# A decoder layer on one core: the next pair's tokens gathered between the halves of an up-projection, x ahead of the weights, more chunks loaded by halves

## The chip, the cores and the metric

The kernel runs on one core of a Trainium2 chip. The metric is the device time of one launch in microseconds. A core has five engines with an instruction queue each: TensorE (PE), VectorE (DVE), ScalarE (ACT), GpSimd (POOL) and SyncE (SP). They run beside each other and wait for each other by semaphores. Data come from the chip's memory (HBM) by DMA; a transfer is issued from an engine's queue, and SP issues nearly all of the weights' here. The kernel before takes 1218.23 us (median of 3 runs, 1218.07 to 1219.96).

## The reference

One decoder layer for 320 tokens of width 1024 in float32: 256 of a prompt and 8 sequences of 8 sample tokens. All tokens share the weights.

```
u = rmsnorm(x, norm1) @ w_in                 # split into q, k, v, GLA parts, gates
oa = sliding-window attention with sinks      # 8 heads of 64, 2 key-value heads
ob = gated linear attention, chunked          # 4 heads, state 64x128 each
merged = sigmoid(g_a) * (oa @ w_a) + sigmoid(g_b) * (gated_norm(ob) @ w_b)
h = x + merged @ w_o
t = rmsnorm(h, norm2)
logits = t @ w_router + b_router              # top 4 of 32 experts, softmax over the four
for each expert e:                            # w1: 1024x2048, w2: 1024x1024
    up = t[rows of e] @ w1[e] + b1[e]
    g, l = min(up[::2], 7), clip(up[1::2], -7, 7)
    y[rows of e] += gate * ((g * sigmoid(1.702 g) * (l + 1)) @ w2[e] + b2[e])
return h + y, and the new caches and states
```

The weights of the 32 experts are 32 x 12.6 MB = 403 MB of the 436 MB that are read.

## The kernel before, in words

**The stages.** First x is squared, turned and normed; 36 projection tiles of `w_in` follow (`project`, L607), with the steps of both mixers between them in an order written out by hand (`between`, L825). Then come the two branch projections (`branch`, L851), the output projection with routing (L967 to L1011), and the expert stage, 32 experts in 16 pairs. Each engine has its own instruction list with the same order of steps; nothing is planned at run time.

**x and the first weights.** SP issues tile 0 of x and the identity, then waits until tile 1 of x has landed (L367) and only then issues the weight units of `w_in`, 1 MB each (`load_unit`, L369). Tiles 1 and 2 of x are issued from ACT's queue (L1255). PE turns the tiles (L589), ACT squares them (L1263), DVE makes the normed, turned `xnT` in eight parts (L1572), and the first projection (L657) needs unit 0 and `xnT`.

**The ring of weights.** SBUF holds a ring of 20 slots of 1 MB. The experts' weights come in 96 chunks of 4 slots (`CHUNKS`, L93): two chunks for a `w1` (h = 0, 1) and one for a `w2`. The ring has five rooms; chunk i goes to room i modulo 5 as soon as chunk i - 5 has been used. A chunk is issued whole (`load_chunk`, L407) when its predecessor has been used whole, or, where `halved(i)` (L103) is true, as two halves of 2 MB, each when the corresponding half of the predecessor has been used (`load_half`, `await_used`). Halved are chunks 0 to 5 and the last one, 95, whose halves come in two pieces each (`load_end`). The order of chunks is w1 of expert 2p, w2 of expert 2p - 1, w1 of 2p + 1, w2 of 2p. PE counts its use in `w1_used` (one per 128 rows of w1) and `w2_used`.

**One pair of experts on PE** (`body`, L1157). Each expert has 64 slots for tokens. `up(2p)` multiplies the pair's tokens `xeT` by w1 in 8 steps k of four matmuls, into PSUM banks 0 and 1 (L1067). `down(2p-1)` is the second projection of the expert before (L1123). `turn(2p)` turns the result for SwiGLU on DVE and ACT (L1082; `swiglu`, L1939). `combine` spreads the pair before's outputs to the tokens by one-hot matrices with the gates in them (L1140), DVE adds them to `acc` (`add`, L1961). Then `up(2p+1)`, two more combines, `down(2p)`, `turn(2p+1)`, `turn_gates` (L1133), and last `gather(p+1)` (L1021): 12 matmuls with one-hot matrices pick the next pair's tokens out of `hn` into PSUM banks 4 and 5 (L953, L955), ACT copies them to `xe` (L1491), PE turns them (`turn_tokens`, L1032; L1039), DVE scales them into `xeT` (`take_tokens`, L1927; L1935). The next `up` waits for these (`xe_ready`). `xe` and `u_sb`, which holds the result of an up-projection, share memory.

**The last pair** (`last_body`) has no gather and ends with `down_end` and `combine_end` by halves of the columns, then the stores.

**b2.** The biases of the second projection are loaded after the states have been stored (L567), by halves into free corners of `acc` and `hn`. In the first pair they take the combine's place (`add_biases`, L1143).

**Attention.** `attend(s)` (L724) multiplies values and probabilities for two key-value heads, whose outputs go to PSUM partitions 0 to 63 and 64 to 127: all of head 0, then all of head 1.

The passes inside `If(busiest > SLOTS)` don't run on these inputs: no expert gets more than 64 tokens, and no loads beyond the 96 chunks stand in the trace.

Of the kernel before, what the change touches and what calls it, by code (L numbers as in the profile page):

```python
# [22 lines left out]
P = 128  # L23
D = 1024
KD = D // P
# [77 lines left out]
def halved(i):  # L103
    return i <= ROOMS or i == len(CHUNKS) - 1
# [53 lines left out]
def layer(nc: bass.Bass, x_prompt, x_sample, cache_k, cache_v, state_gla, norm1, w_in, q_norm, k_norm,  # L158
          sinks, w_gk, b_gk, gla_norm, w_a, w_b, w_o, norm2, w_router, b_router, w1, b1, w2, b2, consts,
          y_prompt, y_sample, k_prompt, v_prompt, s_prompt, k_sample, v_sample, s_sample):  # L160
    with ExitStack() as ctx:
# [93 lines left out]


        b2r = [tile[0:EXPERTS, 2, 512:D] for tile in (acc, hn)]
# [97 lines left out]

        def order_of(f):

            return f // 4 * 4 + f % 2 * 2 + f // 2 % 2
# [157 lines left out]
        def _(pool):  # L516
# [50 lines left out]
            for half in range(2):  # L567
                pool.dma_start(b2r[half], b2[0, :, 512 * half:512 * half + 512]).then_inc(b2_in, 16)
# [3 lines left out]
        def _(pe):  # L572
# [151 lines left out]
            def attend(s):  # L724
                take(N_USES, n_freed, f"attend{s}")
                pe.wait_ge(vw_freed, use(VW_USES, f"probs{s}"))
                for g in range(KVH):
                    out = ps[HD * g:HD * g + HD, NB, :]
                    if s < 4:
                        blocks = [1] if s < 2 else [0, 1]  # L730
                        for kb in blocks:
                            mm = pe.matmul(out[:, 0:256], vA[:, s // 2 - 1 + kb, HD * g:HD * g + HD],
                                           pT[:, kb, 2 * g:2 * g + 2, :].rearrange("p h q -> p (h q)"),
                                           start=(kb == blocks[0]), stop=(kb == 1))
                    else:
                        for hf in range(2):
                            pe.matmul(out[:, P * hf:P * hf + P], vA[0:64, 2, HD * g:HD * g + HD], pT[0:64, 1, 2 * g + hf, :],
                                      start=True, stop=False, skip_group_check=True)
                            for q in range(4):
                                mm = pe.matmul(out[:, P * hf + 32 * q:P * hf + 32 * q + 32],  # L740
# [267 lines left out]
            for t, (_, r) in enumerate(TILES):  # L1008
                mm = pe.matmul(ps[0:1, NB, 96:128], const("ones")[0:r, 0:1], sel[0:r, t, :],
                               start=(t == 0), stop=(t == 2))  # L1010
            mm.then_inc(pos_psum, 1)  # L1011
# [9 lines left out]
            def gather(p, added, gates_copied):  # L1021
# [8 lines left out]
                turn_tokens(p, gates_copied)  # L1030
# [1012 lines left out]
```

## Time and profile before

| | us |
|---|---|
| median of 3 runs | 1218.23 |
| profiled execution, whole | 1217.98 |
| its span, first to last instruction | 1215.9 |
| PE matmuls busy in the span | 1173.4 |
| DVE, ACT, POOL busy | 328.2, 185.6, 28.7 |
| mean rate of the DMA over the span | 362 GB/s |
| rate in most slices after the first expert | 430 GB/s |
| first projection matmul | 12.12 |
| first matmul of up(0) | 296.92 |
| last matmul group begins | 1204.5 |

Times of the trace count from the span's start. A row of grouped instructions gives the engine, the line of the kernel, the operation, its output and input tiles, a count, and in brackets how long the engine was idle before and what ended that. A matmul of float32 shows as two records, each with its weight load (PEld). A DMA row stands at the time of its issue, not of its flow.

### The profile page before, as it was taken

Reading aid. Unit: us, or ns where it says so; the run is one execution under the profiler, and the core shown is the slowest. Engines: PE = TensorE matmul, PEld = TensorE weight load, DVE = VectorE, ACT = ScalarE, POOL = GpSimd, SP = SyncE. Lnnn points to the kernel's source line nnn. Section 1 sums busy time; section 2 is a strip of 40 time slices with the busy share of each in tenths; the row PEclk is TensorE's granted clock in tenths of the full one; section 3 lists DMA queues with packets and bytes.
Section 4 is the critical chain, followed back from the end, with each engine's and each line's share of the span. In section 5 each row is a group of like instructions: output and inputs, shape, how many; then the busy total and the mean of one; then the engine's idle time right before and its main releaser. Section 6 shows DMA issues by size and latency. Waiting matters only on the chain.

```text
span 1215.9 us, 12613 instructions
## 1 busy us (share of the span) xinstructions
PE 1173.4 (97%) x5439; PEld 533.8 (44%) x5439; DVE 328.2 (27%) x668; ACT 185.6 (15%) x339; POOL 28.7 (2%) x54
## 2 busy tenths in 40 slices
PE   7999999999999999999999999999999999899997
PEld 6676678744343433333343433333333333333333
DVE  2406323624222222212122232221221212121222
ACT  2124321002111110101110111111110101010111
POOL 4102000000000000000000000000000000000000
PEclk9999999999999999999999999999999999999999
DMA  9734152975999999999999999999999999999994
GB/s 294 229 122 116 35 139 86 402 291 199 370 398 434 433 430 431 433 431 430 432 433 430 431 431 430 430 431 432 432 431 431 432 430 429 433 432 432 430 423 161
DMA packets 42122, 439.93 MB, mean 362 GB/s; under 512 B 3278, under 2 KB 21040, under 8 KB 28864
## 3 DMA queue, kind: packets, MB, share of 16 engines
q1 hardware_dynamic: 39920, 434.19, 86.0%
q0 software_dynamic: 1904, 4.10, 1.2%
q8 instruction: 45, 0.74, 0.3%
q10 hardware_dynamic: 240, 0.79, 0.2%
q14 instruction: 13, 0.11, 0.0%
HBM read 436.38 MB, written 3.67 MB: 362 GB/s over the span
## 4 chain that ended last, share of the span: by engine, by line
PE 72%; DMA 25%; ACT 1%; DVE 1%; issue 1%; ACTq 0%; DVEq 0%
PE ps L1067 25%; DMA ring<-in_w 24%; PE ps L1123 14%; PE ps L657 9%; PE ps L1140 5%; PE ps L857 3%; PE ps L953 3%; PE ps L877 2%; PE ps L647 1%; PE ps L624 1%; PE ps L1082 1%; PE ps L955 1%; PE ps L776 1%; PE ps L881 1%; PE ps L1093 1%
## 5 line engine op out<-in xcount | busy, mean ns | idle before, releaser
L1067 PE MATMUL ps<-ring,hnT 128*64 128x512 f32 x2040 | 449.7, 598 | 14.2 <-DMA ring<-in_w 13.8
L1067 PEld LDWEIGHTS ps<-ring,hnT 128*64 128x64 f32 x2040 | 150.1, 138 | 299.9 <-issue 277.6
L1123 PE MATMUL ps<-ring,xnT 128*64 128x512 f32 x992 | 218.7, 593 | 4.4 <-DMA ring<-in_w 4.4
L1123 PEld LDWEIGHTS ps<-ring,xnT 128*64 128x64 f32 x992 | 75.0, 137 | 142.5 <-issue 142.3
L1943 DVE TENSOR_TENSOR xnT<-ps,b1T 128x512 f32<-128x512 f32 x32 | 22.1, 691 | 426.5 <-PE ps L1082 426.5
L657 PE MATMUL ps<-xnT,ring 128*128 128x320 f32 x400 | 115.6, 445 | 1.8 <-DMA ring<-in_w_in 1.8
L1459 ACT COPY hnT<-ps 128x1024 f32<-128x1024 f32 x32 | 32.4, 1012 | 481.3 <-PE ps L1067 481.3
L1964 DVE TENSOR_TENSOR acc<-acc,ps 128x1024 f32<-128x1024 f32 x32 | 38.9, 1217 | 222.1 <-PE ps L1140 222.1
L657 PEld LDWEIGHTS ps<-xnT,ring 128*128 128x128 f32 x400 | 76.2, 195 | 35.1 <-issue 3.8
L1140 PE MATMUL ps<-xnT,cst 128*128 128x512 f32 (+1 forms) x180 | 74.4, 618 | 2.7 <-ACT xnT L1472 1.3
L953 PE MATMUL ps<-region,cst 128*128 128x512 f32 x128 | 59.7, 607 | 0.7 <-issue 0.7
L1471 ACT COPY xnT<-ps 64x512 f32<-64x512 f32 x31 | 17.9, 578 | 229.7 <-PE ps L1123 229.7
L1082 PEld LDWEIGHTS ps<-cst,hnT 128*128 128x128 f32 x256 | 33.3, 210 | 28.3 <-issue 23.5
L1140 PEld LDWEIGHTS ps<-xnT,cst 128*128 128x128 f32 (+1 forms) x180 | 23.4, 171 | 43.8 <-issue 37.6
L1082 PE MATMUL ps<-cst,hnT 128*128 128x128 f32 x256 | 39.3, 296 | 2.8 <-ACT hnT L1459 2.8
L953 PEld LDWEIGHTS ps<-region,cst 128*128 128x128 f32 x128 | 22.8, 189 | 34.3 <-issue 34.3
L1935 DVE TENSOR_TENSOR hnT<-ps,n_cols 128x512 f32<-128x512 f32 x32 | 22.0, 691 | 33.8 <-PE ps L1039 33.8
L877 PE MATMUL ps<-ring,xnT 128*128 128x512 f32 x64 | 29.8, 603 | 0.0
L1039 PE MATMUL ps<-cst,hnT 128*128 128x128 f32 x128 | 22.0, 295 | 3.1 <-ACT hnT L1491 3.1
L1491 ACT COPY hnT<-ps 128x512 f32<-128x512 f32 x32 | 18.7, 585 | 40.1 <-PE ps L953 40.1
L1039 PEld LDWEIGHTS ps<-cst,hnT 128*128 128x128 f32 x128 | 19.0, 207 | 13.1 <-issue 7.1
L1465 ACT ACTIVATE sig<-xnT 128x512 f32<-128x512 f32 x32 | 20.1, 630 | 27.5 <-DVE xnT L1947 27.5
(282 smaller groups left out, 730.9 us busy)
## 6 DMA issues: line engine op xcount, KB each, us to landing
ring<-in_w SPq DMA_DIRECT2D x89, 4096.0 KB, 36.5
ring<-in_w SPq DMA_DIRECT2D x10, 2048.0 KB, 15.2
ring<-in_w_in SPq DMA_DIRECT2D x17, 1024.0 KB, 7.9
ring<-in_w SPq DMA_DIRECT2D x7, 1024.0 KB, 19.6
ring<-in_w_o SPq DMA_DIRECT2D x2, 2048.0 KB, 14.4
ring<-in_w_a SPq DMA_DIRECT2D x2, 1024.0 KB, 11.3
ring<-in_w_b SPq DMA_DIRECT2D x1, 2048.0 KB, 15.2
acc<-in_x_prompt SPq DMA_DIRECT2D x3, 512.0 KB, 13.2
```

What stands on the lines that cost most here:

```text
L657: mm = pe.matmul(ps[:, bank, 0:T], unit(m)[:, k, c:c + P], xnT[:, k, :], start=(k == 0), stop=(k == KD - 1))
L857: mm = pe.matmul(ps[:, u % 3, 0:T], w_sb[:, k, P * m:P * m + P], operand[:, k, :], start=(k == 0), stop=(k == 3))
L877: mm = pe.matmul(ps[:, (XB, VB_)[t] + c, :], xnT[:, k, t0:t0 + r], wo_sb[c][:, k, :], start=(k == 0), stop=(k == KD - 1), skip_group_check ...
L953: return pe.matmul(ps[:, XB + half, :], pick[:, t, :], hn[:, t, 512 * half:512 * half + 512], start=start, stop=stop, skip_group_check=True)
L1039: mm = pe.transpose(ps[:, bank, P * k:P * k + P], xe[:, 512 * half + k:512 * half + k + 509:4], ident)
L1067: mm = pe.matmul(ps[o:o + 64, q // 2, :].rearrange("p (j x) -> p j x", x=4), xeT[:, k, SLOTS * which:SLOTS * (which + 1)], columns[:, q], ...
L1082: mm = pe.transpose(ps[:, 2 + gl, o:o + P], u_sb[:, q, 2 * r + gl:2 * r + gl + 509:4], ident)
L1123: mm = pe.matmul(ps[64 * c:64 * c + 64, 6, :], hT[:, which, order_of(f), :], ring[:, slot, D * (f % 2) + 512 * c:D * (f % 2) + 512 * c + 512],
L1140: mm = pe.matmul(out, lhsT, rhs[half], start=True, stop=True)
L1459: nc.scalar.copy(u_sb[:, :, :], ps[:, 0:2, :]).then_inc(u_copied, 1)
L1943: dve.tensor_tensor(glu, ps[:, 2, :].rearrange("p (f t) -> p f t", f=KF), wide(b1T[:, bass.ds(e, 1), 0, :].rearrange("p a f -> p (a f)").u ...
L1964: dve.tensor_tensor(acc[:, t, :], acc[:, t, :], ps[:, bank:bank + 2, :].rearrange("p a b -> p (a b)"), ALU.add).then_inc(comb_added, 1)
```

## The change

- SP issues x tiles 1 and 2 itself, right behind the identity and ahead of the weight units, and doesn't wait; ACT no longer issues them.
- `halved` is true for chunks 0 to 15 and 87 to 95.
- b2 goes to `y_sb` in one transfer, which POOL issues once the first step of up(0) is done.
- `attend` alternates the two heads inside its loops.
- `count_tokens`, three small matmuls that count the tokens of each expert, moves from ahead of up(0) to its middle.
- The gather of pair p + 1 moves from the end of the pair into `up(2p+1)`: ahead of k = 4 the gather, ahead of k = 6 the turning. The tokens of odd pairs go to a second buffer, in the corners of `acc` and `hn` that b2 had. ACT's copies, DVE's scaling and the waits are reordered to it; combine(3p+1) waits for `xe_ready`.
- In the passes that don't run here the loop is unrolled by two.

```diff
 def halved(i):
-    return i <= ROOMS or i == len(CHUNKS) - 1
+    return i <= 3 * ROOMS or i >= len(CHUNKS) - 9
@@ setup
-        b2r = [tile[0:EXPERTS, 2, 512:D] for tile in (acc, hn)]
+        odd_tokens = [tile[:, 2, 512:D].rearrange("p (k s) -> p k s", k=4) for tile in (acc, hn)]
+        b2r = y_sb[0:EXPERTS, :]
+        def tokens_of(odd, k):
+            return odd_tokens[k // 4][:, k % 4, :] if odd else xeT[:, k, :]
@@ SP
-            sp.wait_ge(x_in[1], 16)
+            for t in (1, 2):
+                sp.dma_start(acc[0:TILES[t][1], t, :], x_tile(t)).then_inc(x_in[t], 16)
@@ POOL
-            for half in range(2):
-                pool.dma_start(b2r[half], b2[0, :, 512 * half:512 * half + 512]).then_inc(b2_in, 16)
+            pool.wait_ge(w1_used, 1)
+            pool.dma_start(b2r, b2[0]).then_inc(b2_in, 16)
@@ PE: attend, s < 4 (s = 4 likewise)
-                for g in range(KVH):
-                        for kb in blocks:
-                            mm = pe.matmul(out[:, 0:256], ...)
+                    for kb in blocks:
+                        for g in range(KVH):
+                            mm = pe.matmul(outs[g][:, 0:256], ...)
@@ PE: gather no longer calls turn_tokens; up
-            def up(n, which, again=None, first=False):
+            def up(n, which, odd, again=None, first=False, following=None):
                 if not first:
                     pe.wait_ge(u_copied, n)
                 for k in range(KD):
+                    if first and k == 4:
+                        count_tokens()
+                    if following is not None and k == 4:
+                        gather(*following)
+                    if following is not None and k == 6:
+                        turn_tokens(following[0], None)
...
-                                       xeT[:, k, SLOTS * which:SLOTS * (which + 1)], columns[:, q],
+                                       tokens_of(odd, k)[:, SLOTS * which:SLOTS * (which + 1)], columns[:, q],
@@ PE: body
-                up(2 * p + 1, 1, None if main else again + 1)
+                up(2 * p + 1, 1, odd, None if main else again + 1,
+                   following=(p + 1, 3 * p + 3 if first and not main else 3 * p + 1))
+                pe.wait_ge(xe_ready, 2 * p + 4)
...
-                turn_gates(p)
-                gather(p + 1, 3 * p + 3, p + 1)
+                turn_gates(p, p + 1)
@@ ACT: issues of x 1 and 2 removed; body
-                copy_u(2 * p + 1)
+                copy_xe(p + 1, 2 * p + 1)
+                copy_u(2 * p + 1, turned=2 * p + 4)
                 copy_y(2 * p, 0, 3 * p + 3)
                 copy_gates(p)
                 gate_sigmoid(2 * p + 1)
-                copy_xe(p + 1)
@@ DVE: body
                 swiglu(2 * p, 2 * i, 0, fresh)
                 if not first or main:
-                    for t in range(3):
-                        add(3 * p + t, t, (XB, 0 if last else XB, 2)[t])
+                    add(3 * p, 0)
+                if not last:
+                    take_tokens(p + 1, not odd, second=fresh)
+                if not first or main:
+                    add(3 * p + 1, 1, 0 if last else XB)
+                    add(3 * p + 2, 2, 2)
                 swiglu(2 * p + 1, 2 * i + 1, 1)
-                if not last:
-                    take_tokens(p + 1)
```

## Rows read from the trace of the kernel before

**Rows 1.** The page: busy time of PE, and GB/s in 40 slices.
```profile
PE 1173.4 (97%) x5439; PEld 533.8 (44%) x5439; DVE 328.2 (27%) x668; ACT 185.6 (15%) x339; POOL 28.7 (2%) x54
...
GB/s 294 229 122 116 35 139 86 402 291 199 370 398 434 433 430 431 433 431 430 432 433 430 431 431 430 430 431 432 432 431 431 432 430 429 433 432 432 430 423 161
```

**Rows 2.** The page: shares of the chain that ended last, by engine.
```profile
PE 72%; DMA 25%; ACT 1%; DVE 1%; issue 1%; ACTq 0%; DVEq 0%
```

**Rows 3.** The chain in order of time (start, us, what), one pair's end and start.
```profile
340.52 0.92 PE ps L955 x4
341.43 3.65 PE ps L953 x8
...
345.74 0.75 PE ps L1039 x4
346.49 13.90 PE ps L1067 x64
...
401.72 13.90 PE ps L1067 x64
```

**Rows 4.** Timeline of PE (start, duration, line, count), two waits for weights.
```profile
1061.12 7.09 PE L1067 MATMUL ps<-ring,hnT 128*64 128x512 f32 x32 [2.53 <-DMA ring<-in_w]
...
1119.74 7.09 PE L1067 MATMUL ps<-ring,hnT 128*64 128x512 f32 x32 [2.13 <-DMA ring<-in_w]
```

**Rows 5.** Windows (length, PE, PEld, DVE, ACT, POOL busy, clock, DMA share, GB/s), start.
```profile
4.00:6.00 2.00, 1.13 (x6) 1.11 (x7) 0.42 (x3) 1.15 (x2) 1.44 (x6) 1.00 1.12 398
6.00:8.00 2.00, 2.00 (x11) 1.83 (x10) 0.10 (x2) 1.42 (x4) 0.00 (x0) 1.00 0.30 32
```

**Rows 6.** Timeline of the start, up to the first projection.
```profile
6.78 5.28 SPq L371 DMA_DIRECT2D ring<-in_w_in  x4
...
10.73 3.76 DVE L1572 SCALAR_TENSOR_TENSOR xnT<-ps,cols,hnT 128x320 f32<-128x320 f32 x8
...
12.12 6.14 PE L657 MATMUL ps<-xnT,ring 128*128 128x320 f32 x16 [1.77 <-DMA ring<-in_w_in]
```

**Rows 7.** Windows, the granted clock at the first projection.
```profile
12.00:12.50 0.50, 0.38 (x1) 0.39 (x2) 0.50 (x2) 0.00 (x0) 0.00 (x0) 0.50 1.10 348
```

**Rows 8.** Windows, the granted clock behind attend(4).
```profile
162.10:165.50 3.40, 3.40 (x14) 2.30 (x15) 1.18 (x4) 0.00 (x0) 0.00 (x0) 0.50 1.03 212
```

**Rows 9.** The chain in order of time, attention and projections.
```profile
134.23 1.02 PE ps L732 x8
...
153.81 4.50 PE ps L657 x16
...
158.67 0.58 PE ps L740 x8
...
162.66 5.92 PE ps L657 x16
```

**Rows 10.** The page: DMA issues (count, size, us from issue to landing).
```profile
ring<-in_w SPq DMA_DIRECT2D x89, 4096.0 KB, 36.5
...
acc<-in_b POOLq DMA_DIRECT2D x1, 64.0 KB, 6.6
```

**Rows 11.** Timeline of SP's queue, issues of chunks 7 and 10.
```profile
322.18 0.33 SPq L409 DMA_DIRECT2D ring<-in_w  x1
...
353.55 0.33 SPq L409 DMA_DIRECT2D ring<-in_w  x1
```

**Rows 12.** Windows of 5 us, rate of the stream.
```profile
235.00:240.00 5.00, 5.00 (x20) 3.58 (x19) 2.56 (x6) 0.00 (x0) 0.00 (x0) 1.00 1.00 426
...
320.00:325.00 5.00, 5.00 (x26) 1.61 (x24) 0.00 (x0) 0.00 (x0) 0.00 (x0) 1.00 0.78 275
350.00:355.00 5.00, 5.00 (x26) 1.77 (x24) 0.00 (x0) 0.00 (x0) 0.00 (x0) 1.00 0.85 315
```

**Rows 13.** Windows, the last bytes of the stream.
```profile
1196.00:1198.00 2.00, 2.00 (x14) 0.84 (x12) 0.00 (x0) 0.33 (x1) 0.00 (x0) 1.00 0.29 111
```

**Rows 14.** The chain in order of time, down_end.
```profile
1197.62 6.91 PE ps L1093 x64
```

More of the change, by code:

```diff
@@ L1006, in _, with count_tokens @@
             first_parts(1)
[L1008 to L1011, printed above, removed]
+            def count_tokens():
+                for t, (_, r) in enumerate(TILES):
+                    mm = pe.matmul(ps[0:1, NB, 96:128], const("ones")[0:r, 0:1], sel[0:r, t, :],
+                                   start=(t == 0), stop=(t == 2))
+                mm.then_inc(pos_psum, 1)
             def turn_dense_gates():
@@ L1018, in turn_dense_gates, with gather @@
                 mm.then_inc(gT_psum, 1)
-            def gather(p, added, gates_copied):
+            def gather(p, added):
                 pe.wait_ge(pick_ready, p + 3)
@@ L1139, in spread @@
                     out = ps[:, bank + half, :] if t < 2 else ps[64 * half:64 * half + 64, bank, :]
-                    mm = pe.matmul(out, lhsT, rhs[half], start=True, stop=True)
+                    mm = pe.matmul(out, lhsT, rhs[:, 512 * half:512 * half + 512], start=True, stop=True)
                 mm.then_inc(comb_done, 1)
@@ L1154, in combine, with body @@
                 t0, r = TILES[t]
-                spread(bank, t, gpickT[:, t0:t0 + r], [y_sb[:, 0:512], y_sb[:, 512:D]])
-            def body(p, again=None, loads=None, first=False):
+                spread(bank, t, gpickT[:, t0:t0 + r], y_sb)
+            def body(p, odd, again=None, loads=None, first=False):
                 main = again is None
@@ L1160, in body @@
                 if first:
-                    if main:
-                        turn_tokens(p, None)
-                    else:
-                        gather(p, 3 * p + 3, p)
-                up(2 * p, 0, again, first=fresh)
+                    if not main:
+                        gather(p, 3 * p + 3)
+                    turn_tokens(p, None if main else p)
+                up(2 * p, 0, odd, again, first=fresh)
                 if not first:
@@ L1228, in _ @@
             for p in range(HALF - 1):
-                body(p, first=p == 0)
+                body(p, p % 2 == 1, first=p == 0)
             last_body(HALF - 1)
@@ L1234, in _ @@
                 with pe.Fori(0, PASSES - 1) as b:
[L1235 to L1237 removed]
+                    body(HALF * b + HALF, False, EXPERTS * b, (EXPERTS - 1) * b, first=True)
+                    with pe.Fori(0, HALF // 2 - 1) as i:
+                        for s in (1, 2):
+                            body(HALF * b + HALF + 2 * i + s, s == 1, EXPERTS * b + 4 * i + 2 * s,
+                                 (EXPERTS - 1) * b + 4 * i + 2 * s)
                     last_body(HALF * b + EXPERTS - 1, EXPERTS * b + EXPERTS - 2, (EXPERTS - 1) * b + EXPERTS - 2, b + 1)
@@ L1452, in _, with copy_u @@
                 exps_top(t)
-            def copy_u(n, first=False):
+            def copy_u(n, first=False, turned=None):
                 act.wait_ge(w1_used, KD * n + KD)
+                if turned is not None:
+                    act.wait_ge(xt_done, turned)
                 if not first:
@@ L1494, in body @@
                 if first:
-                    copy_xe(p)
+                    copy_xe(p, None if main else 2 * p)
                 copy_u(2 * p, first=first and main)
@@ L1925, in pick_gates, with take_tokens @@
                 last.then_inc(gpick_ready, 1)
-            def take_tokens(p, fresh=False):
-                if not fresh:
-                    dve.wait_ge(w1_used, 2 * KD * p)
-                else:
+            def take_tokens(p, odd, fresh=False, second=False):
+                if fresh:
                     dve.wait_ge(n2_in, 16)
+                elif not second:
+                    dve.wait_ge(w1_used, 2 * KD * (p - 1))
                 for half in range(2):
@@ L2001, in _ @@
             HALF = EXPERTS // 2
-            body(0, 0, first=True, main=True)
+            body(0, 0, False, first=True, main=True)
             for i in range(1, HALF - 1):
-                body(i, i)
-            body(HALF - 1, HALF - 1, last=True)
+                body(i, i, i % 2 == 1)
+            body(HALF - 1, HALF - 1, True, last=True)
             tail(HALF, 0)
@@ L2013, in _ @@
                     pick_tokens(HALF * b, 0)
-                    body(HALF * b, 0, first=True)
-                    with dve.Fori(1, HALF - 1) as i:
-                        body(HALF * b + i, i)
-                    body(HALF * b + HALF - 1, HALF - 1, last=True)
+                    body(HALF * b, 0, False, first=True)
+                    with dve.Fori(0, HALF // 2 - 1) as i:
+                        for s in (1, 2):
+                            body(HALF * b + 2 * i + s, 2 * i + s, s == 1)
+                    body(HALF * b + HALF - 1, HALF - 1, True, last=True)
                     tail(HALF * b + HALF, 3 * b)
```

51 lines of the change are left out of this document (25 added, 26 removed).

## Prediction

> **What bounds the kernel now.** I read the page first. PE is busy in 9 tenths or more of all slices but a few, and the stream carries 430 GB/s from the twelfth of 40 slices on [rows 1]; the reader should see that two resources look full at once, so busy shares cannot say which one sets the end. The chain says both do, in turn: 72% PE, 25% DMA [rows 2]. So I cut the span into stages.
>
> From 0 to 297 us (mixers, merge, routing) PE works without pause while the DMA often idles; a microsecond off PE there is a microsecond off everything behind it. From 297 us the 32 experts are streamed, 4.19 MB a chunk. PE needs from 346.49 to 401.72 = 55.2 us for a pair of experts [rows 3]. The DMA needs longer: the landings that PE waited for at 1061.12 and 1119.74 are one pair apart, 58.6 us [rows 4], or 9.77 us a chunk. PE starts with five rooms full and has eaten that lead by about 750 us; from there the stream alone sets the pace. Hence three places count: what comes before the first expert; microseconds in which the stream stood still after 300 us; and what PE does after the last chunk it had to wait for, at 1119.74, since from there to the end no wait on the stream longer than a few tenths remains. Anything else that PE saves inside the expert loop is covered by the stream: up to the 58.6 - 55.2 = 3.4 us of slack per pair it costs and brings nothing.
>
> **The change part by part**, against the profiled execution's 1217.98 us (span 1215.9), 0.25 below the median of the three runs.
>
> *x ahead of the weights.* SP waits for tile 1 of x and issues the first weight unit only at 6.78 us; meanwhile the stream drops to 32 GB/s in 6 to 8 us [rows 5]. Unit 0 lands at 12.1 and releases the first projection at 12.12 [rows 6]. Without that wait, SP issues x0, ident, x1, x2 and unit 0 one after another (0.4 us each) by about 2.8 us. That is 1.4 MB of x and ident and 1.05 MB of unit 0: by the 398 GB/s of 4 to 6 us [rows 5] the first is in by about 6.0, by 348 GB/s [rows 7] unit 0 by 9.1. Next late is then xnT: DVE L1572 starts at 10.73 [rows 6] and hands over its first eighth 0.54 us later. It follows from ACT squaring tile 1 at 6.79, where its own chain would allow 6.3 (root of tile 0 done), so 0.45 earlier: first eighth at about 10.8, PE at 10.9. Saved 1.2 us. Bounds: 0.9 (xnT not earlier) to 1.3.
>
> *The clock behind it.* PE sat idle for 1.77 us before 12.12 [rows 6], and the granted clock is 0.50 [rows 7] for 3.4 us from 11.9, its lower level of 1.2 GHz. PE then does about 5.8 records at 0.53 us where it later does them at 0.27, so 1.6 us are lost. With the idle time cut to about 1 us the fall may not come; 0 to 1.7 us, I take 0.8, half. Likewise after attend(4): its small matmuls are followed by 0.50 [rows 8] and a projection of 5.92 us instead of 4.50 [rows 9]. If the shifted stretch escapes, 1.4 us come back; I take 0.5 of 0 to 1.4. The Trainium skill ("TensorE: Matmul & The Clock Gate", What's actually happening) says that what the gate looks at runs freely and does not restart with the kernel; so both would vary from one execution to the next. No row of a single execution can show that. The same page (Part 4, PE-mode transpose) says that transposes don't count as work to the gate; by it PE's transposes before 10 us would help nothing and the first term would be 1.2 alone, 0.8 less in the sum.
>
> *attend by alternating column groups.* attend(2) and (3) take 1.02 us each for 8 records of 256 columns [rows 9]. In up the groups already alternate: 64 records of 512 columns in 13.90 us [rows 3], 0.109 per 256 columns, so 0.87 for eight; at most 0.15 each is to be had. attend(4) takes four times 0.58 for its 8 narrow records [rows 9] and 0.36 for two wider ones, with weight loads as dense as the matmuls. Between -0.3 and 1.3 in all; near the rows of up, 0.3.
>
> *count_tokens into up(0).* Its 0.35 us leave the path to up(0), but come back behind k = 3 of up(0), before most of the releases that pace the stream: 0. DVE's count then waits some 7 us, and behind it pick_gates, pick_tokens and swiglu(0), of which the last has until 313.25: covered. If not, turn(0) moves by what is late.
>
> *b2 after w1_used 1.* Issued at about 299 instead of 204; it took 6.6 us to land [rows 10], its other half 7.0, and is first read at 313.2. Seven microseconds of cover, nothing gained or lost. If it took the 36.5 us that chunks take in a full queue [rows 10], PE would stall some 21 us there, once; but at 299 us nothing else is in flight.
>
> *Chunks 6 to 15 by halves.* Here SP waits only for half a chunk's use. Before, chunk 6 was issued at 310.91, 7 at 322.18, 9 at 338.98 and 10 at 353.55 (two of these four in [rows 11]), for 6, 7 and 10 after the stream had run dry: 272 GB/s around the first, 275 and 315 [rows 12] around the others, against 430 later [rows 1]. Bytes flow about 1.0 us after an issue, 4.87 us a half. After, with up(0) at its old time: chunk 5 ends at 310.5 as before and 6 follows at once, to 320.2; 7 (first half issued two k's earlier, 318.7) to 330.0. But chunk 8 replaces the second half of up(1)'s weights, and up(1) now holds the gather (0.92 + 3.65) and the turn (1.2) [rows 3]: its halves go out at 329.05 + 5.76 = 334.8 and 4.7 before, 330.1. Flow to 340.9. Chunk 9 at 341.3 and 344.7: to 352.1. Chunk 10, whose first half goes out at 349.8, follows at once. Before, it flowed from 354.55. Saved 2.45 us; from there on every later chunk is queued in time (16, the first whole one, is issued at 408 and the stream gets to it at 410.5), so all landings are earlier by 2.5. Bounds: 0 (halves flow no earlier) to 4.8 (all of the old gaps).
>
> *The gather inside up(2p+1).* Per pair PE loses the wait for ACT's copy, 0.2 us; covered by the stream, as is everything that it moves. New waits: comb_added 3p+1 before the gather (add at 316.8 to 318.0, gather at 322: 4 us of room), xe_ready before combine (turns of 1.2 and two takes of 0.69 in the 3.5 us that k = 6 and 7 last). Nobody is late by this account. What is not covered is the last pass. PE waited 2.13 us at 1119.74 for the second half of up(29)'s weights [rows 4], and did the gather afterwards. Now the gather (4.57) starts at 1117.6 and fills the wait: k = 4, 5 at 1122.1, turn, k = 6, 7, end at 1130.3; combine 2.9, down 6.9, turn and gates 1.6: up(30) at 1141.6 instead of 1144.2. Saved 2.6, from the stream's own clock, to the end. The chunk's halves (87) bring nothing more, since the gather covers its landing. The last piece of weights lands at about 1197.4 (the stream thins to 111 GB/s in 1196 to 1198 [rows 13]) and is used by the last of down_end's four steps of 1.73 us, which began at 1202.8 [rows 14] and now begins at 1200.2: the stream doesn't take over. Bounds 0.2 to 4.5.
>
> Sum: 1.2 + 0.8 + 0.5 + 0.3 + 2.45 + 2.6 = 7.85 us; 1217.98 - 7.85 = 1210.1, and 1210.2 beside the median.
>
> **The rivals.** *More of it:* neither fall of the clock, and the early gaps close wholly: 1.2 + 1.7 + 1.4 + 0.3 + 4.8 + 2.6 = 12.0, 1206.0. Against it: the delayed release of chunk 8. *Less of it:* xnT or unit 0 is no earlier, the clock falls as before, or the last wait moves to another place: 2.45 + 2.6 + 0 to 1, so 1212 to 1213. For it: PE's gains at 0 to 20 us hang on arrivals that I have only worked out. *No change:* the stream is set by something that started before 297 us; against it the gaps. *Slower:* 18 chunks more are cut in two, 18 additional boundaries in the one queue that sets the pace. If the stream pauses at each for the 1.0 us between an issue and its first byte, 18 us are added and 7.85 saved: 1228. It decides from 0.44 us per boundary. Against it: in 235 to 240 the stream is made of halves and carries 426 GB/s [rows 12], and transfers take 36.5 us from issue to landing [rows 10], so several stand in the queue at a time. The Trainium skill ("DMA: Bandwidth & Descriptors", Anatomy of one DMA) gives a fixed cost of some 2.0 us per transfer. Taken as serial, that would be an estimate of 36 us more, 1246; the 426 GB/s say that it overlaps.
>
> **How the numbers follow.** Forecast 0.60; more of it 0.12; less of it 0.18; no change 0.05; slower 0.05. What can be told from no change here is about 0.2%, 2.4 us. The forecast's own bounds give 1207.5 to 1212.5; with the cases to both sides, 1205.8 to 1214.0. Faster 0.90, same 0.05, slower 0.05.
>
> **What would show it.** L371's first issue near 2.5 us and the first L657 at about 10.9; the granted clock at 12 and 162 us, each way. Up(0) starting 2 to 3 us earlier. The stream at 300 to 355 without gaps but two of 1.1 and 1.4 us, around 330 and 341. Landings late in the run earlier by the front's gain plus 2.5. PE's wait before k = 4 of up(29) gone, and the end 2.6 us nearer to the last landing than before (now some 18.5). Wrong: any new wait of PE on b2 at L1140, on xe_ready after up, or a stream below 430 GB/s while chunks are halved.

## The result, and the profile after

The changed kernel takes 1215.63 us (median of 17 runs, 1212.41 to 1220.62) where the kernel before takes 1218.74 (17 runs, 1216.99 to 1221.51): a ratio of 0.9975, 95% interval 0.9966 to 0.9984, or 3.1 us. Forecast were 7.85 us and 1210.2, with 1205.8 to 1214.0 as the range. The direction was right, the size more than twice too large, and the time lies outside the range. A second set of 12 runs of the changed kernel on another chip gave 1212.64 and a ratio of 0.9954 (0.9939 to 0.9970).

The profiled execution of the changed kernel took 1216.93 us, its span 1214.7, so 1.2 us less than the span before. The profile page's lines that answer to [rows 1, 2]:

```profile
PE 1179.1 (97%) x5439; PEld 524.8 (43%) x5439; DVE 327.2 (27%) x668; ACT 185.8 (15%) x339; POOL 28.3 (2%) x53
...
GB/s 310 189 145 118 36 139 102 407 238 208 382 398 429 434 431 430 432 430 431 430 431 430 430 431 431 431 430 431 431 431 431 431 431 431 431 430 425 427 426 195
...
PE 76%; DMA 21%; ACT 1%; issue 1%; DVE 1%; SPq 0%; DVEq 0%
```

The steady stream is as before except in slices 37 and 38, where it is now made of halves and carries 425 and 427 GB/s instead of 432 and 430. The chain goes through PE for 76% of the span instead of 72%, through the DMA for 21% instead of 25%. The stages tell more. First the start, which answers to [rows 6]. The timeline's rows are start, duration, engine and line, the operation with its tiles, and in brackets the idle time before it.

```profile
2.76 8.84 SPq L376 DMA_DIRECT2D ring<-in_w_in  x4
...
7.54 3.01 PE L594 MATMUL ps<-cst,acc 128*128 128x128 f32 x16 [0.74 <-DMA acc<-in_x_prompt]
...
12.70 3.76 DVE L1590 SCALAR_TENSOR_TENSOR xnT<-ps,cols,hnT 128x320 f32<-128x320 f32 x8
...
13.39 7.21 PE L662 MATMUL ps<-xnT,ring 128*128 128x320 f32 x16 [1.08 <-DVE xnT L1590]
```

The weights are issued four microseconds earlier, as foreseen, and yet the first projection starts 1.27 us later: tile 1 of x comes at 7.54 instead of 6.8, `xnT` at 12.70 instead of 10.73. The wait's releaser has changed from the weights to `xnT`. The projection takes 7.21 us, since the clock first rises at 18.8. The windows print 1.00 up to there because the trace's first record of the clock stands at the rise; the pace shows the lower level, 2 matmul records in half a microsecond where the kernel before had 4 at the same place:

```profile
16.00:16.50 0.50, 0.50 (x2) 0.31 (x1) 0.46 (x1) 0.00 (x0) 0.00 (x0) 1.00 1.11 352
```
```profile
16.00:16.50 0.50, 0.50 (x4) 0.34 (x3) 0.00 (x0) 0.00 (x0) 0.00 (x0) 1.00 1.10 350
```

The first of these is after, the second before. Unit 0 of the weights, foreseen at 9.1 us, lands at 11.49 by its semaphore, against 12.07 before. While x and the weights arrive the DMA carries less than the 348 to 398 GB/s that the prediction reckoned with:

```profile
5.00:6.00 1.00, 1.00 (x6) 1.00 (x7) 0.42 (x3) 0.58 (x3) 0.52 (x1) 1.00 0.80 288
6.00:7.00 1.00, 0.80 (x4) 0.40 (x2) 0.00 (x0) 0.09 (x1) 0.00 (x0) 1.00 1.07 217
7.00:8.00 1.00, 0.46 (x2) 0.46 (x3) 0.00 (x0) 0.48 (x1) 0.00 (x0) 1.00 1.09 255
```

Attention, in the chain in order of time (start, us, what), answers to [rows 9]:

```profile
136.58 1.01 PE ps L737 x8
...
160.65 0.37 PE ps L743 x4
161.02 0.59 PE ps L747 x16
161.61 0.36 PE ps L743 x4
161.97 0.59 PE ps L747 x16
...
162.94 4.50 PE ps L662 x16
...
203.53 1.75 PE ps L804 x16
205.28 0.49 PE ps L800 x4
205.77 2.53 PE ps L804 x16
208.30 6.96 PE ps L864 x16
```

attend(4) takes 1.91 us instead of 3.77: 16 records now take the time of 8. The projection after it is at full pace (4.50). But the branch projection at 208 takes 6.96 us. In the kernel before it was:

```profile
208.66 4.40 PE ps L857 x16
```

The windows, as in [rows 7, 8], show the granted clock: 1.00 behind attend(4), 0.50 from 206.5 on. From 185.4 to 206.5 PE was busy for all 21.1 us; just ahead of the fall (last window) matmuls and weight loads both ran without a pause.

```profile
162.10:165.50 3.40, 3.40 (x34) 2.58 (x31) 1.18 (x4) 0.00 (x0) 0.00 (x0) 1.00 1.02 210
206.60:213.20 6.60, 6.60 (x19) 4.83 (x19) 1.89 (x2) 2.99 (x4) 0.00 (x0) 0.50 1.03 364
```
```profile
204.00:206.00 2.00, 2.00 (x20) 2.00 (x20) 0.00 (x0) 0.00 (x0) 0.00 (x0) 1.00 0.96 262
```

up(0) starts at 298.65 us, 1.73 later than before. The early stream, against [rows 12]:

```profile
320.00:325.00 5.00, 5.00 (x26) 1.52 (x22) 0.29 (x1) 0.00 (x0) 0.00 (x0) 1.00 0.99 416
325.00:330.00 5.00, 5.00 (x18) 1.87 (x16) 0.00 (x0) 1.17 (x2) 0.00 (x0) 1.00 1.00 419
330.00:335.00 5.00, 5.00 (x28) 2.15 (x26) 1.29 (x2) 0.00 (x0) 0.00 (x0) 1.00 0.81 298
...
340.00:345.00 5.00, 5.00 (x24) 1.63 (x24) 1.16 (x2) 0.00 (x0) 0.00 (x0) 1.00 0.95 380
...
350.00:355.00 5.00, 5.00 (x26) 1.68 (x24) 4.03 (x13) 0.34 (x1) 0.00 (x0) 1.00 1.01 433
```

The gaps of before (275 and 315 GB/s) are gone, and the two foreseen new ones are there (298 and 380 GB/s; foreseen around 330 and 341 from the old start of up(0), so 332 and 343 here). Last, the tail, against [rows 4]; the first row is before, the second after:

```profile
1100.26 7.09 PE L1123 MATMUL ps<-ring,xnT 128*64 128x512 f32 x32 [0.80 <-DMA ring<-in_w]
```
```profile
1101.08 7.09 PE L1137 MATMUL ps<-ring,xnT 128*64 128x512 f32 x32 [1.16 <-DMA ring<-in_w]
```
```profile
1118.43 1.06 PE ps L962 x4
1119.49 3.63 PE ps L960 x8
1123.12 3.58 PE ps L1081 x16
1126.71 1.16 PE ps L1046 x8
1127.87 3.58 PE ps L1081 x16
1131.45 2.92 PE ps L1154 x8
...
1142.83 13.91 PE ps L1081 x64
```

Both rows are the wait for chunk 85. In the changed kernel it is the last wait for weights, and after it comes up(29) with the gather (L962, L960) and the turn (L1046) inside. PE no longer waits for chunk 87, as it did at 1119.74 [rows 4]. From chunk 85's release to the end of the span it is 113.6 us, before (1100.26 to 1215.9) 115.6.

### The profile page after: what moved, and what is told of

Read it like the earlier page. It is cut to its first block, busy times and chain, and to the rows that moved or that the text cites. A ratio compares the mean times of both kernels' runs of the same rounds, so it can differ in the third digit from the quotient of the medians.

```text
span 1214.7 us, 12644 instructions
## 1 busy us (share of the span) xinstructions
PE 1179.1 (97%) x5439; PEld 524.8 (43%) x5439; DVE 327.2 (27%) x668; ACT 185.8 (15%) x339; POOL 28.3 (2%) x53
## 4 chain that ended last, share of the span: by engine, by line
PE 76%; DMA 21%; ACT 1%; issue 1%; DVE 1%; SPq 0%; DVEq 0%
PE ps L1081 27%; DMA ring<-in_w 20%; PE ps L1137 14%; PE ps L662 9%; PE ps L1154 5%; PE ps L864 3%; PE ps L960 3%; PE ps L884 2%; PE ps L652 1%; PE ps L1096 1%; PE ps L629 1%; PE ps L1046 1%; PE ps L962 1%; ACT xnT L1488 1%; PE ps L783 1%
## 5 line engine op out<-in xcount | busy, mean ns | idle before, releaser
L1081 PE MATMUL ps<-ring,hnT 128*64 128x512 f32 x1016 | 225.5, 595 | 0.0
L1081 PEld LDWEIGHTS ps<-ring,hnT 128*64 128x64 f32 x1016 | 70.7, 137 | 140.1 <-issue 138.6
L1081 PE MATMUL ps<-ring,region 128*64 128x512 f32 x512 | 114.6, 595 | 1.1 <-DMA ring<-in_w 1.1
L1081 PE MATMUL ps<-ring,acc 128*64 128x512 f32 x512 | 113.4, 595 | 0.3 <-DVE acc L1986 0.3
L1154 PE MATMUL ps<-xnT,cst 128*128 128x512 f32 (+3 forms) x192 | 79.3, 617 | 2.7 <-ACT xnT L1488 1.3
L1081 PEld LDWEIGHTS ps<-ring,region 128*64 128x64 f32 x512 | 36.2, 137 | 72.0 <-issue 71.1
L1081 PEld LDWEIGHTS ps<-ring,acc 128*64 128x64 f32 x512 | 35.4, 137 | 70.3 <-issue 69.3
L960 PE MATMUL ps<-region,cst 128*128 128x512 f32 x128 | 59.7, 606 | 0.7 <-issue 0.7
L1096 PEld LDWEIGHTS ps<-cst,hnT 128*128 128x128 f32 x256 | 33.3, 210 | 28.3 <-issue 23.5
L1509 ACT COPY hnT<-ps 128x512 f32<-128x512 f32 x32 | 18.8, 586 | 172.4 <-PE ps L960 172.4
L1154 PEld LDWEIGHTS ps<-xnT,cst 128*128 128x128 f32 (+3 forms) x192 | 24.9, 170 | 46.5 <-issue 40.1
L1096 PE MATMUL ps<-cst,hnT 128*128 128x128 f32 x256 | 39.4, 297 | 2.9 <-ACT hnT L1475 2.9
L960 PEld LDWEIGHTS ps<-region,cst 128*128 128x128 f32 x128 | 22.8, 189 | 34.3 <-issue 34.3
```

The lines of the kernel that those rows point to most:

```text
L960: return pe.matmul(ps[:, XB + half, :], pick[:, t, :], hn[:, t, 512 * half:512 * half + 512], start=start, stop=stop, skip_group_check=True)
L1081: mm = pe.matmul(ps[o:o + 64, q // 2, :].rearrange("p (j x) -> p j x", x=4), tokens_of(odd, k)[:, SLOTS * which:SLOTS * (which + 1)], colu ...
L1096: mm = pe.transpose(ps[:, 2 + gl, o:o + P], u_sb[:, q, 2 * r + gl:2 * r + gl + 509:4], ident)
L1154: mm = pe.matmul(out, lhsT, rhs[:, 512 * half:512 * half + 512], start=True, stop=True)
L1509: nc.scalar.copy(xe[:, 512 * half:512 * half + 512], ps[:, XB + half, :]).then_inc(xe_copied, 1)
```

## The experiments

Four numbers of each trace are compared in the table: when tile 1 of x is turned; when the first projection starts and its last record begins; when up(0) starts; and when chunks 10, 16 and 85 have arrived, counted from up(0). A chunk's arrival is worked out from the DMA packets of SP's queue: the moment at which the bytes still to come are those of the chunks behind it. PE's release for chunk 85 comes 3.0 to 4.3 us after that moment (before: 1100.26 against 1096.7), in e1 5.5, so the column serves for comparing traces and not as a time of landing. "Low clock" lists the stretches at 0.50 before up(0), behind the first rise; they last 3.4 us where no other length stands beside them. Each row is one profiled execution. The edits are shown abridged; a comment or a line "@@" stands for what is left out.

| trace | tile 1 | first projection | first rise; low clock | up(0) | chunk 10, 16, 85 |
|---|---|---|---|---|---|
| before | 6.83 | 12.12, 17.82 | 8.5; 11.9, 162.1 | 296.92 | 69.1, 127.3, 799.8 |
| after | 7.54 | 13.39, 20.17 | 18.8; 206.5 (6.8 us) | 298.65 | 67.1, 126.2, 798.9 |
| e1 | 6.74 | 12.01, 17.71 | 8.4; 11.8 | 292.83 | 68.1, 126.9, 799.5 |
| e2 | 8.95 | 14.81, 21.12 | 19.3; 210.4 | 300.28 | 69.2, 127.5, 799.9 |
| e3 | 6.90 | 12.01, 16.13 | 9.6; 204.1 | 292.94 | 71.5, 129.6, 802.2 |
| e4 | 6.78 | 12.01, 17.84 | 8.6; 12.0 | 293.44 | 69.2, 127.4, 800.0 |
| e5 | 7.98 | 13.84, 20.64 | 19.3; 207.0 (6.8), 295.8 | 300.75 | 67.0, 126.2, 798.8 |
| e6 | 8.30 | 14.16, 20.66 | 19.0; 210.1 | 299.81 | 69.1, 127.4, 799.9 |
| e7 | 6.96 | 14.31, 20.37 | 8.0; 11.4 (6.8) | 295.50 | 67.0, 126.2, 798.8 |
| e8 | 6.96 | 12.82, 19.33 | 17.7; 205.4 (6.8) | 297.80 | 65.8, 126.6, 799.2 |
| e9 | 8.43 | 14.29, 20.34 | 18.2; none | 295.47 | 67.3, 126.3, 798.9 |
| e10 | 6.73 | 12.58, 18.68 | 16.6; 204.3 (6.8) | 297.14 | 67.0, 126.3, 798.8 |
| e11 | 7.33 | 12.57, 19.72 | 8.5; 11.9 (6.8), 206.4 (6.8), 295.2 | 299.78 | 65.5, 125.3, 797.6 |
| e12 | 7.96 | 13.81, 19.64 | 17.3; none | 294.77 | 67.0, 125.9, 803.8 |
| e13 | 7.83 | 13.69, 19.61 | 17.3; none | 294.74 | 67.1, 126.2, 798.9 |
| e14 | 7.48 | 13.35, 18.90 | 16.3; none | 294.02 | 67.2, 126.3, 798.9 |

**e1, the old start of x in the changed kernel.**
```diff
-            for t in (1, 2):
-                sp.dma_start(acc[0:TILES[t][1], t, :], x_tile(t)).then_inc(x_in[t], 16)
+            sp.wait_ge(x_in[1], 16)          # and ACT issues tiles 1 and 2 again
```


> The changed kernel with the old start: tiles 1 and 2 of x from ACT's queue, SP waiting for tile 1. Theory A (issuing x from SP and the weights right behind it made tile 1 land late, at 7.54 instead of 6.8 us, since unit 0's packets run beside it, and the first xnT late, 12.70 instead of 10.73): tile 1 lands near 6.8, the first projection starts at 12.1 to 12.3, up(0) starts 1.5 to 2.5 us earlier than the changed kernel's 298.65, and the time is 1 to 2.5 us below the changed kernel's. Theory B (the late start of that one trace was the clock's chance and has nothing to do with x's queue): tile 1's landing stays near 7.5 or varies either way, and up(0)'s start differs only by falls of the clock.

Tile 1 at 6.74 and the first projection at 12.01 are as theory A has them; up(0) at 292.83 is earlier than it has it. The times don't bear it out: 1215.68 us over 10 runs, ratio to before 0.9962 (0.9947 to 0.9977), an interval that overlaps the changed kernel's. Of up(0)'s 5.8 us, 2.5 are the start and 3.35 the low clock at 206 us that this trace doesn't have.

**e2, x ahead alone, in the kernel before.** The diff is the change's own, on SP and ACT.

> The kernel before with x ahead of the weights as the only edit. Theory A (x lands later behind SP's third and fourth issue and beside unit 0): the first projection starts at 13.0 to 13.5 instead of 12.12 us, and the time is 1 to 2.4 us above before. Theory B (chance): the first projection starts at 11 to 12.1 and the time is 0 to 2 us below before, as was predicted.

Tile 1 at 8.95, first projection at 14.81, later even than foreseen. The profiled execution took 1223.82 us. But the median of the 12 runs is 1217.06, ratio 0.9990 (0.9978 to 1.0002), most of them near 1216.3 and one other near 1223.8. For the start theory A holds in this trace; for the time, neither slower nor faster is shown.

**e3, the old halving in the changed kernel.**
```diff
-    return i <= 3 * ROOMS or i >= len(CHUNKS) - 9
+    return i <= ROOMS or i == len(CHUNKS) - 1
```


> The changed kernel with the old halving (chunks 0 to 5 and 95). Theory A (halves close early gaps worth 2.0 us up to chunk 10, and then cost 0.1 us a chunk, 1.0 by chunk 16 and 0.5 in the last nine): chunk 10 comes 2 us later against up(0)'s start than in the changed kernel, in fact more, since the gather in up(1) delays the release of chunk 9 by 5.8 us: 2 to 5 us later; the time 1 to 4 us above the changed kernel. Theory B (halves bring nothing): chunk 10 at the same distance from up(0), time within 0.5 us.

1219.57 us over 12 runs, ratio 1.0004 (0.9989 to 1.0018): without the added halves the change, 0.9975 with them, shows no gain. Chunk 10 arrives 4.4 us later than in the changed kernel and 2.4 later than before; chunk 85 3.3 and 2.4. The stream from 330 us, in windows:

```profile
330.00:335.00 5.00, 5.00 (x18) 1.34 (x16) 1.36 (x2) 1.01 (x1) 0.00 (x0) 1.00 0.58 197
335.00:340.00 5.00, 5.00 (x26) 1.72 (x24) 0.46 (x1) 0.00 (x0) 0.00 (x0) 1.00 1.00 429
340.00:345.00 5.00, 5.00 (x29) 2.36 (x27) 2.12 (x4) 2.22 (x4) 0.00 (x0) 1.00 0.90 347
```

At 197 GB/s the stream waits for chunk 3's room, in which up(1) still computes because the gather stands in its middle. So the gather inside up(1), with the 0.35 us of count_tokens inside up(0), costs the stream 2.4 us, and the halves win 3.3 net. Theory A. Its profiled execution took only 1214.38: there the last record of the first projection began at 16.13 us and the low clock at 204 lasted 3.4. Its runs fall in two groups with different mean granted clocks: three from 1214.4 to 1214.6 us at 0.995, nine from 1218.2 to 1223.1 at 0.991 to 0.993.

**e4, alternating heads alone, in the kernel before.** The diff is the change's own in `attend`.

> The kernel before with attend alternating the heads as the only edit. Theory A (the narrow matmuls of attend(4) are bound by their weight loads, and loads of one column group run beside those of the other): attend(4) takes 1.9 us instead of 3.8, attend(2) and (3) stay at 1.0; if the clock falls nowhere new, 1.9 us off everything behind, up(0) at 295.1 or, without the fall of the clock at 162 us, at 293.6. Theory B (the gain came from somewhere else in the changed kernel): attend(4) stays at 3.8 and the time at before's.

attend(4) takes 1.9 us, the rest of attention is as it was; in the chain:

```profile
158.31 0.37 PE ps L738 x4
158.68 0.59 PE ps L742 x16
159.27 0.37 PE ps L738 x4
159.63 0.59 PE ps L742 x16
160.22 0.38 PE ps L756 x8
160.60 4.50 PE ps L657 x16
```

up(0) at 293.44, as theory A has it without the low clock at 162 us. 1217.11 us over 12 runs, ratio 0.9989 (0.9972 to 1.0007): 1.9 us at the median, which the interval does not part from nothing.

**e5 and e6, the changed kernel and x ahead alone, one more look each.**

> The changed kernel once more, one look at its start. Theory A (with x on SP's queue one of the 16 DMA engines ends its part of x late, in every execution): tile 1 of x turned from 7.3 us or later, the first projection at 13 us or later. Theory B (it is late only in some executions): tile 1 near 6.3 to 6.8, the first projection at 11 to 12 us.

> The kernel before with x ahead alone, once more. The timed executions of it had most times near 1216.3 and two near 1223.8, and the traced one was among the latter, with tile 1 at 8.95 us. Theory A (always late): tile 1 from 7.3 us on again. Theory B (late in some): tile 1 near 6.5, the first projection below 12 us, time near 1216.3.

Tile 1 at 7.98 and at 8.30: late again in both, theory A. (e3, which also has x on SP's queue, has 6.90, so it isn't late in every execution.) 1218.89 and 1219.97 us, single runs.

**e7, x on ACT's queue, SP not waiting.**
```diff
-            for t in (1, 2):
-                sp.dma_start(acc[0:TILES[t][1], t, :], x_tile(t)).then_inc(x_in[t], 16)
+                                             # no wait; ACT issues tiles 1 and 2 again
```


> The changed kernel with tiles 1 and 2 of x issued from ACT's queue as before, and SP not waiting for them: the weights' first unit is issued at about 1.7 us. Theory A (unit 0's packets beside x are what makes x late): tile 1 lands at 7.5 us or later here too, since they compete from 2.5 us on, and the time is at or above the changed kernel's. Theory B (being third in SP's queue makes it late): tile 1 at 6.8 and the first projection at 11.8 or earlier; 1 us or more below the changed kernel.

Neither as a whole. Tile 1 is early (6.96) although the weights flow beside it, but tile 2, second in ACT's queue, starves beside the weights:

```profile
10.54 0.71 PE L591 MATMUL ps<-cst,acc 64*128 64x64 f32 x8 [2.02 <-DMA acc<-in_x_sample]
...
14.31 5.96 PE L659 MATMUL ps<-xnT,ring 128*128 128x320 f32 x14 [1.08 <-DVE xnT L1589]
```

The first projection waits for it until 14.31. Still 1213.39 us over 12 runs, 0.9962 (0.9947 to 0.9976).

**e8, the first pair's gather back at its end, fewer halves, old start of x.**
```diff
-    return i <= 3 * ROOMS or i >= len(CHUNKS) - 9
+    return i <= 2 * ROOMS + 1 or i == len(CHUNKS) - 1
@@ PE, first pair only; ACT and DVE accordingly
-                   following=(p + 1, ...))
-                pe.wait_ge(xe_ready, 2 * p + 4)
+                   following=None)
+                turn_gates(p, p); gather(p + 1, 3 * p + 3); turn_tokens(p + 1, p + 1)
```


> The changed kernel with the old start of x, the first pair's gather back at the end of the pair (later pairs keep it inside the up-projection), and halves only for chunks 0 to 11 and 95. Theory A (the gather in up(1) delays the release of chunks 8 and 9 by 5.8 us and thereby the stream, halves cost 0.1 us a chunk where no gap is left): chunk 10 at 66 to 67 us from up(0)'s start instead of 67.1 to 68.1, chunk 16 at 124.5 to 125.5 instead of 126.2 to 126.9, and 1 to 2 us below the kernel with the old start of x alone. Theory B (the release isn't what holds the stream there): the same distances as in the changed kernel, and the same time within 0.5 us.

Chunk 10 at 65.8, where theory A has 66 to 67: 1.3 us earlier than in the changed kernel. Chunk 16 at 126.6, not 124.5 to 125.5. One window shows why:

```profile
385.00:390.00 5.00, 5.00 (x28) 2.10 (x25) 1.29 (x2) 0.00 (x0) 0.00 (x0) 1.00 1.00 433
390.00:395.00 5.00, 5.00 (x20) 1.59 (x18) 1.13 (x1) 1.01 (x1) 0.00 (x0) 1.00 0.78 288
```

The stream runs dry once more, and does so where the second pair's gather stands and chunks from 12 on come whole; e11 below, with halves up to 15, doesn't have the loss (chunk 16 at 125.3). 1213.97 us over 12 runs, 0.9962 (0.9949 to 0.9976).

**e9 and e10, the changed kernel and the old start of x, side by side.**

> The changed kernel, timed beside the next two on one chip. Theory A (x on SP's queue lands late): tile 1 turned from 7.3 us on, first projection at 13 us or later, and 1 to 2 us above the kernel with the old start of x. Theory B (the start differs only by chance): the two alike within 0.5 us.

> The changed kernel with the old start of x, timed beside the changed kernel on one chip. Theory A: tile 1 at 6.7 to 7.0 us, 1 to 2 us below the changed kernel. Theory B: alike within 0.5 us.

1212.64 and 1214.72 us (ratios 0.9954 and 0.9960, intervals nearly the same). Tile 1 at 8.43 and 6.73, as theory A has it, but the time is not worse for it: the medians lie 2.1 us apart, the changed kernel's being the lower, within runs that spread from 1210.6 to 1218.3. A's 1 to 2 us are not there; B's "within 0.5 us" is nearer by the ratios (0.0006, some 0.7 us) and not shown by the medians.

e1 and e10 are one program with one start (tile 1 at 6.74 and 6.73), and the clock first rises at 8.35 in one and 16.61 in the other. For that alone `xnT` begins at 10.61 or 11.89 and the last record of the first projection at 17.71 or 18.68. In e9's trace the clock stays up where it fell in the first trace of the same kernel; the same windows:

```profile
206.60:213.20 6.60, 6.60 (x31) 5.01 (x31) 3.03 (x5) 2.99 (x4) 0.00 (x0) 1.00 1.04 365
```

31 matmul records where the trace at 0.50 has 19.

**e11, as e8 with halves up to chunk 15.**
```diff
+    return i <= 3 * ROOMS or i == len(CHUNKS) - 1
```


> Old start of x, the first pair's gather at the end of the pair, halves for chunks 0 to 15 and 95. Theory A (chunks 12 to 15 need their halves too, since whole ones let the stream run dry once more by 1.9 us between chunks 11 and 16): chunk 10 at 65.8 us from up(0)'s start, chunk 16 at 124.9 instead of 126.6, chunk 85 at 797.6; 1.3 us below the kernel with the old start of x. Theory B (the stream's distance at chunk 16 is set by something else): 126.2 or more, as in the changed kernel, no gain.

Chunks at 65.5, 125.3 and 797.6 us from up(0): theory A. The stream is 1.3 us ahead of the changed kernel's at chunk 85. 1214.38 us over 12 runs, 0.9957 (0.9942 to 0.9973): no better than the changed kernel in time that these runs can tell.

**e12, all chunks by halves.**
```diff
+    return True
```


> The changed kernel with all chunks by halves. Theory A (a half's descriptors of 16 KB take 0.615 us where one of 32 KB takes 1.218, so a chunk takes 0.10 us longer): from chunk 16 to 85 the stream takes 679 to 680 us instead of 672.7, and the time is 6 to 8 us above the changed kernel's. Theory B (the longer time of chunks 10 to 16 was not the halves'): 672.7 us, same time. Theory C (each boundary costs the 1.0 us from issue to first byte): 740 us.

From chunk 16 to 85 the stream takes 803.8 - 125.9 = 677.9 us instead of 672.7: 0.075 us a chunk. 1219.45 us over 12 runs, 1.0003 (0.9989 to 1.0016), 6.8 above the changed kernel beside it (e9). The steady stretch:

```profile
400.00:800.00 400.00, 399.26 (x1761) 145.24 (x1760) 98.09 (x197) 51.53 (x80) 0.00 (x0) 1.00 1.01 427
```

Against 431 GB/s in the changed kernel. Theory A, somewhat smaller; C, a pause of 1.0 us at each boundary, is out.

**e13 and e14, x on SP's queue, the weights held back; the same kernel twice.**
```diff
             for t in (1, 2):
                 sp.dma_start(acc[0:TILES[t][1], t, :], x_tile(t)).then_inc(x_in[t], 16)
+            sp.wait_ge(x_in[1], 16)
```


> The changed kernel with x still issued from SP's queue, but SP waiting for tile 1 before the first weight unit. Theory A (the weights right behind x are what makes x late): tile 1 turned at 6.2 to 6.9 us, and the last packets of x end by 6.6. Theory B (one queue for all of x is what makes it late): 7.3 us or later with nothing beside it, the first projection then at 13 us or later since unit 0 is issued only at 7.3.

> The same kernel once more. Theory A: tile 1 at 6.2 to 6.9 us again. Theory B: 7.3 us or later again.

```profile
7.80 5.38 SPq L377 DMA_DIRECT2D ring<-in_w_in  x4
...
7.83 3.01 PE L595 MATMUL ps<-cst,acc 128*128 128x128 f32 x16 [0.82 <-DMA acc<-in_x_prompt]
...
13.69 6.35 PE L663 MATMUL ps<-xnT,ring 128*128 128x320 f32 x16 [1.08 <-DVE xnT L1591]
```

Tile 1 at 7.83 and 7.48 with no weights in flight: theory B. The late x doesn't need the weights as neighbours; what these traces share with the other late ones is the one queue for all of x. Whether the weights add to it (8.3 to 9.0 in e2, e6 and e9) is not shown. And the weights, issued 5 us later than in the changed kernel, don't delay the first projection: unit 0 lands at 13.12, `xnT` releases PE at 13.69. 1212.84 us over 5 runs, 0.9955 (0.9935 to 0.9975).

## Why the prediction was right and wrong

The span before and two spans of the changed kernel, cut at the same places, give what each part of the sum became (us saved against the span before):

| part | foreseen | after | e9 |
|---|---|---|---|
| to the last record of the first projection (x ahead, first fall of the clock) | 2.0 | -2.35 | -2.52 |
| from there to up(0) (second fall of the clock, attend, count_tokens) | 0.8 | 0.62 | 3.97 |
| up(0) to chunk 85 (halves) | 2.45 | 0.9 | 0.9 |
| chunk 85 to the end (gather in up(29)) | 2.6 | 2.05 | 2.7 |
| whole span | 7.85 | 1.2 | 5.05 |

**x ahead and the clock at the start (foreseen 1.2 and 0.8 us saved): the step that failed.** Both arrivals in it were worked out from a rate and not bounded from above; no value beyond "xnT not earlier" stood in the bounds. Tile 1 of x was to be squared by ACT at 6.3 and was squared at 7.52 and turned at 7.54; it is turned at 7.5 to 9.0 in eight of the nine traces with x on SP's queue and at 6.7 to 7.3 in the seven others, whose tile 1 ACT issues. e13 and e14 point to the queue as the cause. Unit 0 was to land at 9.1 and landed at 11.49 (11.5 to 12.9 in the seven traces that issue it right behind x), so with xnT as early as foreseen no more than 0.6 of the 1.2 us was to be had. e3 had tile 1 at 6.90 and an early clock, and its first projection starts at 12.01, 0.1 us before the old one.

The larger part is the clock. The sum took its early rise (8.5 us in the trace of before) for given and asked only whether the fall at 11.9 would come. In the profiled pair the rise itself came at 18.8. `xnT` begins 1.97 us later: 0.71 are tile 1's, and 1.26 come from the steps behind it, which take 5.16 us in after and e10, at the lower clock, and 3.90 in before. The projection, which in before ran in part at each level, takes 1.08 us more from its first record to its last (6.78 instead of 5.70). Against that stand 0.70 us that PE had waited for unit 0: 0.71 + 1.26 + 1.08 - 0.70 = 2.35. Over many runs the late tile 1 doesn't show in the time: e9's median is below e10's.

**The second fall of the clock (foreseen 0.5 us saved).** The fall at 162 us went, but one at 206.5 came. What a fall costs can be read from the table of the experiments: from the last record of the first projection to up(0) it is 275.1 us in e1, e7, e9, e12, e13 and e14, which have none between, 278.5 in after, e8 and e10 with 6.8 us of low clock, 276.8 in e3 with 3.4 us. So 3.35 and 1.7 us. In after the 0.62 us of this stretch are then 1.9 of attend, 0.35 of count_tokens and 1.7 of the fall that went, less 3.35 of the one that came; e9 has the gains alone. The same program has it (after, e5) or not (e9). The forecast took half a gain; right was a spread, 3.35 us in after, 5.0 in e5 and nothing in e9 from one program, and no trace shows that the change steers it. The mean granted clock of each run fits this beyond the traces: e8 has six runs from 1211.1 to 1212.4 us at 0.995 to 0.996 and six from 1215.6 to 1216.5 at 0.992 to 0.994, with none between; e9 has eight up to 1213.7 at 0.995 to 0.997 and four above at 0.992 to 0.994. In the 17 runs of the changed kernel the two groups overlap (1212.4 to 1217.6 at 0.995 and above, 1213.6 to 1220.6 below), so there the clock is not all; such a mean also holds falls in the expert stage and behind chunk 85 (e11 and e14 have one there).

**attend (0.3 us): too small.** 1.9 us, all in attend(4), and beyond my upper bound of 1.3. The bound from the rows of up was right for attend(2) and (3), 0.01 us. That attend(4)'s weight loads are as dense as its matmuls stood in the text, but I drew the wrong sum from it: 16 loads of 0.138 us each now stand in 0.55 us, where 8 stood in 0.54. So loads into alternate column groups overlap more; that they are what held the records back is the likely reading, and no run parts it from the matmuls' own pace.

**count_tokens (0), b2 (0): right.** The three matmuls stand inside up(0) (0.35 us): they are off the way to up(0) and on the way to the stream's releases. No wait on b2 appears.

**Halves, early (2.45 us): the mechanism right, the size not.** Chunk 10 comes 2.0 us earlier against up(0). By chunk 16 it is 1.1 and at chunk 85 0.9. The halves' lower rate was not in the sum: e12 measures 0.075 us a chunk, so 0.4 us for chunks 11 to 15. The rest of what is lost between chunks 10 and 16 stays open. "A stream below 430 GB/s while chunks are halved" was one of the signs of being wrong, and it came.

**The gather in up(29) (2.6 us): right, a little too large.** 2.0 us from chunk 85's release to the end; PE's wait for chunk 87 is gone.

**The rivals.** "Slower" at 1.0 us a boundary is out by e12, but some cost was real: 0.075 us. The 2.0 us that the prediction took from the Trainium skill ("DMA: Bandwidth & Descriptors", Anatomy of one DMA) stand there for transfers that GpSimd issues, and SP issues these; e12's 69 further transfers cost 5.2 us in all. "Less of it" is nearest: the move of the wait from the weights to `xnT` and a clock no better than before came true. Its 1212 to 1213 was still too low for the 1215.63, since it had nothing on the side of loss.

The 3.1 us of the medians is more than the profiled pair shows, and e9's 5.8 more again. How the levels of the clock spread over untraced runs, and why x ahead alone (e2) is no slower in them, stays open. That the sum's gains in attend, the halves and the tail are there in the medians as in the traces is argued and not shown part by part: e4 alone is not parted from nothing. No version tried beats the changed kernel beyond its interval.

## What to carry to other kernels

Work moved between the first and second use of a buffer delays that buffer's refill by all of its length; where the stream is not yet saturated this costs, unless the refill goes out in parts. Parts have a price in the steady stream, so cut only the chunks behind which it would run dry. An arrival that no trace shows needs a bound on the late side too, also when its transfer only changes queues. And where one program has the clock at either level in the same place, a single trace of it is one draw: forecast the spread, and compare stretches that no fall touches.

## What the runs showed of the hardware

- Tiles of x issued one after another on one queue mostly end late: the last packets of x at 7.6 to 8.9 us in eight traces of nine, with the weights beside them or not (e13: 7.98), against 6.85 to 7.3 where ACT issues tiles 1 and 2 and SP waits. The Trainium skill ("DMA: Bandwidth & Descriptors", Queues, rings and completion order) says that SP and ACT each have a row of rings on the same 16 engines; that x over two rows ends earlier would fit, but no run here tells why.
- A chunk as two transfers of 16 KB per partition instead of one of 32 KB takes about 0.075 us more of 9.75.
- 16 narrow matmul records (32 columns) take 0.59 us when they alternate between two column groups, 1.17 when they don't; 8 records of 256 columns take 1.01 and 1.02.
- The clock fell at 206.5 us in after although PE had been busy without a gap since 185.4; 3.4 us at the lower level cost 1.7 us there, 6.8 us 3.35.
- In the kernel before the clock rose at 8.5 us after nothing but transposes. The Trainium skill ("TensorE: Matmul & The Clock Gate", PE-mode transpose) says that these don't count as work; here they did. In e10 the same transposes ran from 4.85 to 9.7 us and it rose only at 16.6. That what the gate looks at does not restart with the kernel (same page of the Trainium skill, What's actually happening) fits both this and after and e9, one program with and without the fall.
